# A recurrence's convolution read straight from PSUM, and four steps of ScalarE and TensorE moved by some chunks

## The reference, cut to what matters

```python
def causal_dwconv(x, w, b):
    S = x.shape[1]
    xp = jnp.pad(x, ((0, 0), (CONV_K - 1, 0), (0, 0)))      # CONV_K = 4
    y = xp[:, 0:S, :] * w[0]
    for k in range(1, CONV_K):
        y = y + xp[:, k:k + S, :] * w[k]
    return y + b

def rglru_branch(u, gate, ...):
    xc = causal_dwconv(u, conv_w, conv_b)
    r = sigmoid(xc by heads @ w_rg + b_rg)     # 16 blocks of 128 x 128
    i = sigmoid(xc by heads @ w_ig + b_ig)
    log_a = -8 * r * softplus(-lam)
    a, mult = exp(log_a), sqrt(-expm1(2 * log_a))
    h = scan(a, mult * i * xc)                 # h_t = a_t h_(t-1) + b_t
    return (h * silu(gate)) @ w_o

merged = sigmoid(m_mla) * y_mla + sigmoid(m_lru) * y_lru
q = rms_norm(q_lat, q_a_norm) @ w_q_b          # and the same for kv_lat: "the latents"
```

## Time and profile before

| | |
|---|---|
| three runs | 1988.18 us median |
| the profiled execution | 1989.17 us, its span 1987.4 us |
| TensorE (PE) busy | 1953.0 us, 98% of the span |
| VectorE (DVE) busy | 1083.2 us, 55% |
| ScalarE (ACT) busy | 785.4 us, 40% |
| GpSimd (POOL) busy | 620.6 us, 31% |
| mean granted TensorE clock | 0.995 of full speed |

### The profile page before, as it was taken

One profiled execution on the slowest core, in us unless ns is written; L12 is line 12 of the kernel. 1 busy time (PEld: TensorE's weight loads), 2 busy tenths in 40 slices (PEclk: granted clock), 3 DMA queues, 4 the chain that ended last, 5 costly groups with the idle time before them and its releaser, 6 DMA issues.

```text
span 1987.4 us, 27817 instructions
## 1 busy us (share of the span) xinstructions
PE 1953.0 (98%) x10798; PEld 1708.9 (86%) x10798; DVE 1083.2 (55%) x1571; ACT 785.4 (40%) x1259; POOL 620.6 (31%) x463
## 2 busy tenths in 40 slices
PE   7999999999999999999999999999999999999996
PEld 6889999999998887887788888888888888888885
DVE  4867778788883584587856557661011330111444
ACT  6434444444443446446345545422222222333323
POOL 3000000000003454454452223254444454444452
PEclk9999999999999999999999999999999999999998
DMA  6444444444445333334352334253333443225232
GB/s 245 129 137 127 135 132 126 134 126 137 128 128 172 105 116 123 131 106 143 94 150 86 127 106 149 81 216 107 126 116 127 137 170 104 88 87 210 86 105 106
DMA packets 210727, 256.26 MB, mean 129 GB/s; under 512 B 20749, under 2 KB 144309, under 8 KB 203061
## 3 DMA queue, kind: packets, MB, share of 16 engines
q1 hardware_dynamic: 195792, 185.11, 30.4%
q10 hardware_dynamic: 14821, 69.56, 9.3%
HBM read 218.45 MB, written 33.55 MB: 127 GB/s over the span
## 4 chain that ended last, share of the span: by engine, by line
issue 70%; POOL 26%; PE 1%; DVE 1%; POOLq 1%; ACT 1%; DMA 0%; ACTq 0%; DVEq 0%
POOL wlo L420 26%; PE ps L1544 1%; POOLq L419 1%; DMA ropec<-in_rope_const 0%; ACT hhi L486 0%; POOLq L429 0%; DVE x L1533 0%; DVE hlo L1055 0%; DVE sqj L1037 0%; ACT xraw L467 0%; DVE x L1506 0%; DVE stage L1505 0%; DVE x L1536 0%; ACT whi L445 0%; POOL wlo L427 0%
## 5 line engine op out<-in xcount | busy, mean ns | idle before, releaser
L420 POOL TENSOR_TENSOR wlo<-raw,whi 128x512 fp32r<-128x512 f32 x448 | 614.2, 1375 | 1328.8 <-ACT whi L445 1327.8
L445 ACT ACTIVATE whi<-raw 128x512 fp32r<-128x512 f32 x480 | 299.7, 631 | 777.7 <-PE ps L1544 727.9
L1544 PE MATMUL ps<-hhi,whi 128*128 128x512 f32 x640 | 250.0, 391 | 2.1 <-POOL wlo L420 2.1
L1544 PE MATMUL ps<-hlo,whi 128*128 128x512 f32 x640 | 249.1, 389 | 0.0
L1544 PE MATMUL ps<-hhi,wlo 128*128 128x512 f32 x640 | 249.0, 389 | 0.0
L1651 PE MATMUL ps<-shi,cut 128*128 128x256 f32 x768 | 217.3, 283 | 0.0
L1652 PE MATMUL ps<-slo,cut 128*128 128x256 f32 x768 | 217.3, 283 | 0.0
L1653 PE MATMUL ps<-shi,cut 128*128 128x256 f32 x768 | 217.3, 283 | 0.0
L573 ACT ACTIVATE cut<-wblock 128x768 fp32r<-128x768 f32 x96 | 81.1, 845 | 270.8 <-PE ps L1653 270.3
L1652 PE MATMUL ps<-hlo,cut 128*128 128x256 f32 x576 | 163.0, 283 | 0.0
L1653 PE MATMUL ps<-hhi,cut 128*128 128x256 f32 x576 | 163.0, 283 | 0.0
(11 more groups left out here) (284 smaller groups left out, 4141.1 us busy)
## 6 DMA issues: line engine op xcount, KB each, us to landing
wblock<-in_w_in SPq DMA_DIRECT2D x384, 128.0 KB, 2.5
raw<-in_w_in SPq DMA_DIRECT2D x40, 1024.0 KB, 5.0
raw<-in_w_o_lru SPq DMA_DIRECT2D x16, 1024.0 KB, 5.0
raw<-in_w_o_mla SPq DMA_DIRECT2D x16, 1024.0 KB, 5.0
raw<-in_w_out SPq DMA_DIRECT2D x16, 1024.0 KB, 5.0
raw<-in_w_ple_gate SPq DMA_DIRECT2D x16, 1024.0 KB, 5.0
gate_scr<-stage ACTq DMA_DIRECT2D x16, 512.0 KB, 3.5
raw<-in_w_kv_b SPq DMA_DIRECT2D x32, 256.0 KB, 4.0
```

The lines of the kernel that those rows point to most:

```text
L420: pool.tensor_tensor(wlo[:, k % RING], raw[:, k // RAWC, k % RAWC], whi[:, k % RING].bitcast(F32), ALU.subtract).then_inc(lo_ready, 1)
L445: act.activation(whi[:, c % RING], raw[:, c // RAWC % 2, c % RAWC], ACT.Copy).then_inc(hi_ready, 1)
L1544: return pe.matmul(o, l, r, start=start, stop=stop)
```

## The change

Nothing that is computed changes. There are four edits:

1. The copy into `upad` is gone. The convolution reads the PSUM banks directly: the first instruction takes the tap without a delay over all 512 columns, and three more add the columns shifted by 1, 2 and 3, which are 511, 510 and 509 long. The set is given back after the convolution of all four banks, not before it. The low part `gwlo` stands ahead of the convolution, and the four `xclo` behind it. The freed place in SBUF is called `mult`, for what stood in `upad` later on.
2. The gates and the ScalarE work with `d` = 4 have `d` = 2: TensorE runs `gates(1, 0)` and `gates(3, 0)` after chunk 7 of `C_M2` and of `C_LAT` (before: 9), and pair 1 after chunk 10 (before: 12). The sigmoids of pair 0 stand one chunk earlier in `lru_work`.
3. The merge gate of `C_M2` stands behind ScalarE's second split of the group `C_U[2]` (before: ahead of its first).
4. The sum of the squares and the `krw` matmuls stand after chunk 9 of `C_LAT + KD` (before: 12). ScalarE's steps for the latents stand one to four chunks earlier.

```diff
@@ lru_work (ScalarE) @@
-                if k == 2 + d:
-                    lru_x(i, 0)
+                if k in (1 + d, 2 + d):
+                    lru_x(i, k - 1 - d)
                 if k == 3 + d:
-                    lru_x(i, 1)
+                    lru_x(i, 2)
+                    lru_x(i, 3)
                 if k == 5 + d:
-                    lru_x(i, 2)
+                    lru_sigmoids(i, 0)
                 if k == 6 + d:
-                    lru_x(i, 3)
-                    lru_sigmoids(i, 0)
-                if k == 7 + d:
                     lru_tanh(i, 0)
                     lru_gate_in(i)
@@ ScalarE, groups C_M2 and C_U[2] @@
-                lru_work(1, k, 4)
-            act.wait_ge(z_stored, 16 * UNITS)
-            merge_gate_out(0, 1, U_M2, sig_stored)
+                lru_work(1, k, 2)
             for k in range(KD):
                 split(C_U[2] + RING + k)
-                if k == 8:
+                if k == 1:
+                    act.wait_ge(z_stored, 16 * UNITS)
+                    merge_gate_out(0, 1, U_M2, sig_stored)
+                if k == 5:
                     lru_out(1)
@@ ScalarE, groups C_LAT and C_LAT + KD @@
-                lru_work(3, k, 4)
+                lru_work(3, k, 2)
...
-                if k == 6:
+                if k == 5:
                     act.wait_ge(krw_landed, 16)
                     act.activation(krw2[:, :, 0:QK_ROPE], krw[:], ACT.Copy).then_inc(krw_hi, 1)
-                if k == 8:
+                if k == 4:
                     lru_out(3)
                     squares(latq, 0)
-                if k == 10:
+                if k == 6:
                     act.wait_ge(angle_ready, 1)
...
-                if k == 12:
+                if k == 9:
                     root(TT + 1)
-                if k == 13:
+                if k == 10:
                     latent_hi(latq, qlhi, 0)
-                if k == 14:
+                if k == 12:
                     act.wait_ge(kr_done, 1)
@@ VectorE, the convolution @@
             for i in range(NG):
                 s = SET_U[i]
+                dve.wait_ge(gw_hi, i + 1)
+                step(dve.tensor_tensor(gwlo[:], graw[:, 4 * i:4 * i + 4], gwhi[:].bitcast(F32), ALU.subtract))
+                signal(gw_lo)
                 dve.wait_ge(chunk_used, C_U[i] + KD)
                 for m in range(4):
-                    step(dve.tensor_copy(upad[:, m, 3:], ps[:, 4 * s + m]), wait=m == 3)
-                signal(released[s])
-                for m in range(4):
...
-                    step(dve.tensor_scalar(xc[:, m], upad[:, m, 0:S], tap(0), vec[:, V_CB + 4 * i + m:V_CB + 4 * i + m + 1],
-                                           ALU.mult, ALU.add))
-                    for n in range(1, 4):
-                        step(dve.scalar_tensor_tensor(xc[:, m], upad[:, m, n:n + S], tap(n), xc[:, m], ALU.mult, ALU.add))
+                    u = ps[:, 4 * s + m]
+                    step(dve.tensor_scalar(xc[:, m], u, tap(3), vec[:, V_CB + 4 * i + m:V_CB + 4 * i + m + 1], ALU.mult, ALU.add))
+                    for late in range(1, 4):
+                        step(dve.scalar_tensor_tensor(xc[:, m, late:], u[:, 0:S - late], tap(3 - late), xc[:, m, late:], ALU.mult, ALU.add))
                     signal(xc_ready)
-                    if m == 1:
-                        dve.wait_ge(gw_hi, i + 1)
-                        step(dve.tensor_tensor(gwlo[:], graw[:, 4 * i:4 * i + 4], gwhi[:].bitcast(F32), ALU.subtract))
-                        signal(gw_lo)
-                    if m % 2:
-                        for t in (m - 1, m):
-                            dve.wait_ge(xc_hi, 4 * i + t + 1)
-                            lo_of(xclo[:, t], xc[:, t], xchi[:, t]).then_inc(xc_lo, 1)
-                dve.wait_ge(ri_ready, 8 * i + 8)
+                signal(released[s])
                 for t in range(4):
+                    dve.wait_ge(xc_hi, 4 * i + t + 1)
+                    lo_of(xclo[:, t], xc[:, t], xchi[:, t]).then_inc(xc_lo, 1)
+                for t in range(4):
+                    if t % 2 == 0:
+                        dve.wait_ge(ri_ready, 8 * i + 2 * t + 4)
                     step(dve.tensor_tensor(ii[:, t], ii[:, t], xc[:, t], ALU.mult), wait=t == 3)
@@ TensorE @@
-            whole_group(C_M2, 1, U_M2, 1, 4)
+            whole_group(C_M2, 1, U_M2, 1, 2)
...
-            whole_group(C_LAT, 0, U_LAT[0], 3, 4)
+            whole_group(C_LAT, 0, U_LAT[0], 3, 2)
...
                 chunk(C_LAT + KD + k, features, 1, hhi[:, k], hlo[:, k], k, KD)
-                if k == 12:
+                if k == 9:
                     claim(0, U_LAT[0] + 1)
                     square_sum(0, 1)
```

More of the change, by code:

```diff
@@ L182, in trunk_layer @@
         _, swhole, _ = lay(("seven_r12", [P, R1 + R2], F32), ("swhole", [P, 4, KD // 2, H], F32), ("whole_pad", [P, 8], F32))
-        _, gg, upad, _, xc, xchi, xclo, rr, ii, _, graw, gwhi, gwlo = lay(
+        _, gg, mult, xc, xchi, xclo, rr, ii, _, graw, gwhi, gwlo = lay(
             ("lru_r1", [P, R1], F32), ("gg", [P, 4, S], F32),
-            ("upad", [P, 4, S + 3], F32), ("upad_pad", [P, P - 16], F32), ("xc", [P, 4, S], F32), ("xchi", [P, 4, S], F32R),
+            ("mult", [P, 4, S], F32), ("xc", [P, 4, S], F32), ("xchi", [P, 4, S], F32R),
             ("xclo", [P, 4, S], F32R), ("rr", [P, 4, S], F32), ("ii", [P, 4, S], F32),
-            ("lru_pad", [P, R2 - 4 * S - P - 24 * S], F32),
+            ("lru_pad", [P, R2 - 28 * S], F32),
             ("graw", [P, KD, 2 * P], F32), ("gwhi", [P, 4, 2 * P], F32R), ("gwlo", [P, 4, 2 * P], F32R))
-        _, _, _, _, _, asq = lay(
-            ("sq_r1", [P, R1], F32), ("sq_gg", [P, 4, S], F32), ("sq_upad", [P, 4, S + 3], F32),
-            ("sq_pad", [P, P - 16], F32), ("sq_xc", [P, 4, S], F32), ("asq", [P, 4, S], F32))
+        _, _, _, _, asq = lay(
+            ("sq_r1", [P, R1], F32), ("sq_gg", [P, 4, S], F32), ("sq_mult", [P, 4, S], F32),
+            ("sq_xc", [P, 4, S], F32), ("asq", [P, 4, S], F32))
         (_, qlhi, qllo, kvhi, kvlo, cosT, sinT, latq, latkv, tsw, krz, tmp, krw, krw2, posi, _, krhi, krlo0, krlo1) = lay(
@@ L613, in lru_tanh @@
                 for t in (2 * pair, 2 * pair + 1):
-                    act.activation(upad[:, t, 3:], rr[:, t], ACT.Tanh, scale=sp8[:, 4 * i + t:4 * i + t + 1]).then_inc(tanh_ready, 1)
+                    act.activation(mult[:, t], rr[:, t], ACT.Tanh, scale=sp8[:, 4 * i + t:4 * i + t + 1]).then_inc(tanh_ready, 1)
             def lru_decay(i):
@@ L629, in lru_root @@
                     act.wait_ge(var_ready, 4 * i + t + 1)
-                    act.activation(upad[:, t, 3:], upad[:, t, 3:], ACT.Sqrt).then_inc(mult_ready, 1)
+                    act.activation(mult[:, t], mult[:, t], ACT.Sqrt).then_inc(mult_ready, 1)
             def lru_gate_in(i):
@@ L775, in _ @@
                         act.dma_start(tsw[head_rows(1 - e)], krz[head_rows(e)]).then_inc(halves_swapped, 16)
+                if k == 14:
+                    act.wait_ge(kr_summed, 1)
+                    swap_quadrants(tmp[:, 4], tsw, 0)
             for n in range(KD + 2 * KL):
@@ L779, in _ @@
                 split(c + RING)
-                if n == 0:
-                    act.wait_ge(kr_summed, 1)
-                    swap_quadrants(tmp[:, 4], tsw, 0)
                 if n == 1:
@@ L1199, in _ @@
             signal(sp_ready)
-            step(dve.memset(upad[:, :, 0:3], 0.0))
             for i in range(NG):
                 s = SET_U[i]
+                dve.wait_ge(gw_hi, i + 1)
+                step(dve.tensor_tensor(gwlo[:], graw[:, 4 * i:4 * i + 4], gwhi[:].bitcast(F32), ALU.subtract))
+                signal(gw_lo)
                 dve.wait_ge(chunk_used, C_U[i] + KD)
-                for m in range(4):
-                    step(dve.tensor_copy(upad[:, m, 3:], ps[:, 4 * s + m]), wait=m == 3)
-                signal(released[s])
                 for m in range(4):
@@ L1230, in _ @@
                     dve.wait_ge(decay_ready, 4 * i + t + 1)
-                    dve.scalar_tensor_tensor(upad[:, t, 3:], asq[:, t], 1.0, upad[:, t, 3:], ALU.add,
+                    dve.scalar_tensor_tensor(mult[:, t], asq[:, t], 1.0, mult[:, t], ALU.add,
                                              ALU.mult).then_inc(var_ready, 1)
@@ L1235, in _ @@
                     dve.wait_ge(mult_ready, 4 * i + t + 1)
-                    step(dve.tensor_tensor(ii[:, t], ii[:, t], upad[:, t, 3:], ALU.mult))
+                    step(dve.tensor_tensor(ii[:, t], ii[:, t], mult[:, t], ALU.mult))
                     step(dve.tensor_tensor_scan(xc[:, t], rr[:, t], ii[:, t], 0.0, ALU.mult, ALU.add))
```

## The result

The changed kernel takes 1997.55 us, the median of six runs (1995.49 to 1997.93), against 1987.74 us before (six runs, 1986.6 to 1988.99): a ratio of 1.0047, 95% interval 1.0034 to 1.006. It is 9.8 us slower.

A forecast was written before the change was run, and what follows sets the result against it. TensorE, busy 98% of the span, bounds the kernel, so only its waits and clock count. -0.4 - 2.0 + 2.4 + 2.4 + 0.9 = +3.3 us gives a median of 1991.5 us; range 1983.5 to 1998.0, the forecast's own 1984.5 to 1997.7.

The forecast's parts named there:

- The mechanism: C_M2 and C_LAT: TensorE waits 4.4 us ahead of pair 0 for VectorE, slower clock behind; +2.4 us per group.
- the banks are not ready in time: Denies the rival that VectorE gives the banks back in time and all five waits go: -10.8 us, 1977.4; chance 0.15.
- the wait does not merely move: Denies the rival that pair 1's 2 us wait only moves to pair 0, same clock: -2.4 us, 1985.8; chance 0.10.
- Merge gate, -2.0 us: C_U[2]: TensorE's wait at chunk 4 goes once the gate stands behind the second split; -2.0 us, or 0.
- Sigmoids, -0.4: Beside C_U[1]: sigmoids one chunk earlier bring the group from 49.37 to 48.96 us, -0.4 us.
- End of the scan stage, 11.1 us into the group: VectorE's scan stage of the quarter before ends 11.1 us after C_M2 begins (before: 11.4).
- gwlo: VectorE's low part ahead of the convolution: 1.22 us, up to 2.33, with 0.15 us idle on either side.
- The convolution from PSUM, 0.69 us for the first instruction of a bank, no row over 0.76: VectorE in C_M2 and C_LAT: 3.2 us per bank, 12.8 for four, bounds 12.0 to 16.
- The clock, 1.7 us per group: Lowered clock behind TensorE's wait in C_M2 and C_LAT: 1.7 us each, bounds 0 to 3.4 (two slow stretches).
- The rival with two stretches: C_M2 and C_LAT: wait of 6.6 us, two half-clock stretches, +6.3 us each; +11.1 in all, 1999.3; chance 0.09.
- The latents, +0.9 us: C_LAT + KD: TensorE waits 1.9 us against 0.9, +1.0 (-0.9 to +2.7), less 0.1 at the group's end.
- The rule on copying first: Trainium skill's rule against edit 1; forecast: four PSUM reads are cheaper; if the rule held, sum 3.6 us higher.

The follow-up runs named there:

- merge_only: The kernel before with only the merge gate moved behind the second split of C_U[2]: 1985.1 us, ratio 0.9985.
- the first trace: The profiled execution of the changed kernel, 1996.03 us; two more traces of the same kernel took 1997.83 and 1996.49 us.
- lat_undone: The changed kernel with the latents' steps and square_sum put back after chunk 12: 1993.0 us, ratio 1.0025.
- d2_only: The kernel before, with its copy and convolution from SBUF, and only d changed from 4 to 2 for C_M2 and C_LAT: 1988.9 us, ratio 1.0004.
- conv_only: The kernel before with only VectorE's part of the change (no copy, convolution from PSUM, gwlo first, xclo last): 1982.0 us, ratio 0.9974.
- d3: The changed kernel with d = 3 (pair 0 after chunk 8) and the latents where they stood before: 1984.2 us, ratio 0.9983.
- narrow_low: The changed kernel with GpSimd's low part of a chunk cut from 512 to 32 columns from C_U[1] on, result not the reference's: 1978.1 us, ratio 0.9949.

## Why the prediction was right, and where it was too small

The mechanism was the one forecast, and its rivals fell: the banks are not ready in time, and the wait does not merely move. The sum was too small by more than half, +3.3 against +7.9 in the trace and +9.8 by the medians. Step by step:

- *Merge gate, -2.0 us*: right, in the changed kernel and in `merge_only`. *Sigmoids, -0.4*: right, C_U[1] takes 48.96 us.
- *End of the scan stage, 11.1 us into the group*: 11.1 us. *gwlo* took 1.23 us, the lower of the bounds that were kept.
- *The convolution from PSUM, 0.69 us for the first instruction of a bank, no row over 0.76*: it takes 0.81 us. The nearest row had immediate operands, this form has pointers to them; no run varies that alone, so the cause of the 0.12 us is open. Four times 0.12 us and 0.1 us more idle time ahead of `xclo` make the wait 5.1 us from start to start (4.9 of idle time) instead of 4.4. The SCALAR_TENSOR_TENSOR, 0.75 us and never lengthened, was right.
- *The clock, 1.7 us per group*: this is a term that failed. C_M2 lost 1.7 us in the first trace and 2.0 and 2.4 in the others, C_LAT 2.8 to 3.0 in all three. The forecast had "two such stretches" as its upper bound and chose one; in five of six cases (six of eight with `lat_undone`) a wait of 4.9 us drew 6.8 us of slow clock. The rival with two stretches had 0.09, and its clock was nearer to the truth than the forecast's, though not its wait (6.6 us). Its time, 1999.3 us, is 1.8 from the measured one, the forecast's 6.
- *The latents, +0.9 us*: the second term that failed. The waits are 0.9 and 1.6 us from start to start against 0.9 in all before, +1.7 and not +1.0. The forecast then took no clock for them, though it had just priced one behind a wait of 2 us: 3.41 us of slow stretch follow here too, 1.6 us. Less the 0.1 us at the group's end, this makes +3.2, beyond this term's own upper bound of +2.7.
- *The rule on copying first*: the trace decides for the change. Reading PSUM costs 0.81 - 0.55 = 0.26 us more per bank, and the copy was 0.6 to 0.68. The larger part was not in this comparison: from SBUF the convolution is lengthened as well. In `d2_only` the first two banks of C_M2 took 3.97 and 3.96 us each (724.55 to 728.52 to 732.48, with the copy apart), in the changed kernel every bank 3.32 (722.59 to 725.90).

With the measured 5.1 us of wait, 2.8 us of clock and the latents' 3.2, the forecast's own sum is +9.1 us, far on the side of slower.

That the range held the time is in part luck. It needed both groups near their upper bounds, and the upper end itself was added up wrong: -0.4 - 2.0 + 5.2 + 5.2 + 2.7 is +10.7 and not +9.5, which would be 1998.9 us and not 1997.7. Two smaller slips change nothing here: 27.2 us is the place after ten chunks, not nine, and four banks at 3.7 instead of 3.2 us are 2.0 us more, not 1.8.

## What to carry to other kernels

- When TensorE's queue holds work for a side computation, put it by the lengths that the other engine has in the trace while its neighbours run, lengthened rows included. Here twelve instructions that take 10.6 us beside short ones of GpSimd took 17.4 beside its full ones, and those 6.8 us were more than the two chunks (5.4 us) by which the gates were moved.
- A wait of TensorE costs more than its idle time: add 1.7 us for a slow stretch behind one of 2 us about every second time (four of the eight waits of 1.7 to 2.2 us in the traces of before, `merge_only`, `conv_only` and `d3`), and up to 3 us behind one of 5, and do it for each wait in the sum, the small ones too.
- Of an edit in several parts, time each part, and each beside the others. Two of the four here were worth something by themselves (the convolution 6.4 us, the merge gate 3.3). The shifts of a few chunks in the two others turned a gain of 9 us into a loss of 10, and the one that did most of it had cost 0.5 us on the old convolution.

## What the runs showed of the hardware that was not expected

- Equal waits do not bring equal clocks. Of the two waits of 2.2 us in `d3` one was followed by a slow stretch and the other not, and in `d2_only` the longer wait, 3.4 us in C_M2, passed at a clock of 1.00, while the shorter, 3.0 us in C_LAT, brought 6.8 us at 0.50.
- In the trace of `narrow_low` the granted clock reads 0.949 all the way to its last 14 us, and yet its groups take the same 48.96 us as at 1.00. A matmul of 512 columns starts every 0.227 us in both, and every 0.427 at 0.50. If the array alone set the pace, half of 0.427 or 0.214 us would be expected at 1.00 and 0.225 at 0.949 (an estimate from the rows at 0.50), and both are under 0.227. So something other than the granted clock seems to set the pace near full clock; no run shows what.
- A TENSOR_SCALAR of 512 columns took 0.55 us from SBUF with operands by pointer, 0.69 from PSUM with immediate operands, and 0.81 from PSUM with operands by pointer.
